# Eleven small rows packed into one array: one transfer in place of eleven

## The reference

```python
m = jax.nn.silu(c) @ w_mod[l] + b_mod[l]
sh1, sc1, g1, sh2, sc2, g2 = jnp.split(m[:, None, :], N_MOD, axis=-1)
mc = jax.nn.silu(c_ctx) @ w_mod[l] + b_mod[l]
...
hx = modulate(x, norm_attn_pre[l], sh1, sc1)      # rms_norm(x, g) * (1 + scale) + shift
hc = modulate(ctx, norm_attn_pre[l], csh1, csc1)
px = hx @ w_in[l]
pc = hc @ w_in[l]
...
x = x + g1 * rms_norm(mix_x, norm_attn_post[l])
hx2 = modulate(x, norm_ffn_pre[l], sh2, sc2)
yx = moe(...)
x = x + g2 * rms_norm(yx, norm_ffn_post[l])
```

## Time and profile before

| what | value |
|---|---|
| median of 3 runs | 1950.54 us |
| lowest and highest | 1948.37, 1951.08 us |
| the profiled execution's time | 1948.93 us |
| its span, first to last instruction | 1947.0 us |
| TensorE busy | 1855.7 us (95%) |
| VectorE, ScalarE busy | 392.5 us (20%), 343.6 us (18%) |
| moved by the DMA engines | 558.16 MB, mean 287 GB/s |

### The profile page before, as it was taken

The page is one execution under the profiler, slowest core; times in us unless marked ns, Lnnn a source line. Parts: engine busy times, 40 slices in busy tenths (PEclk is TensorE's granted clock), DMA queues, the critical chain, the costliest instruction groups (busy, mean ns, idle before and its releaser), DMA issues. The chain is left out here.

```text
span 1947.0 us, 21918 instructions
## 1 busy us (share of the span) xinstructions
PE 1855.7 (95%) x8913; PEld 1054.1 (54%) x8914; DVE 392.5 (20%) x818; ACT 343.6 (18%) x675; POOL 5.3 (0%) x10
## 2 busy tenths in 40 slices
PE   6999799999999999999999997999999999999998
PEld 4757333333333333333333335768888886786664
DVE  1754411011101111111110114542000033110001
ACT  2222311111111111111111113332000032120001
POOL 0000000000000000000000000000000000000000
PEclk9999799999999999999999999999999999999999
DMA  9984399999999999979999999434244413314331
GB/s 393 310 208 156 150 422 428 429 427 430 427 430 428 429 429 427 429 307 429 428 429 427 430 425 312 164 129 172 102 173 172 167 49 130 130 44 173 124 135 65
DMA packets 100582, 558.16 MB, mean 287 GB/s; under 512 B 16600, under 2 KB 33469, under 8 KB 73789
## 3 DMA queue, kind: packets, MB, share of 16 engines
q1 hardware_dynamic: 98084, 553.09, 70.0%
q10 hardware_dynamic: 2458, 4.50, 1.8%
HBM read 552.34 MB, written 5.23 MB: 286 GB/s over the span
## 5 line engine op out<-in xcount | busy, mean ns | idle before, releaser
L1285 PE MATMUL ps<-ring,xs 128*64 128x512 f32 x2112 | 472.4, 594 | 28.4 <-DMA ring<-in_w_up 17.4
L1285 PEld LDWEIGHTS ps<-ring,xs 128*64 128x64 f32 x2112 | 148.5, 137 | 340.6 <-issue 269.2
L1337 PE MATMUL ps<-ring,actT 128*64 128x512 f32 x1056 | 233.9, 595 | 0.0
L1993 PE MATMUL ps<-hT,ring 128*128 128x256 f32 x1024 | 223.9, 379 | 0.2 <-ACT hT L1522 0.2
L1993 PEld LDWEIGHTS ps<-hT,ring 128*128 128x128 f32 x1024 | 194.5, 190 | 29.5 <-issue 2.9
L1337 PEld LDWEIGHTS ps<-ring,actT 128*64 128x64 f32 x1056 | 72.9, 137 | 158.7 <-issue 131.9
L1788 PE MATMUL ps<-hT,ring 128*128 128x256 f32 x512 | 120.2, 391 | 5.8 <-ACT hT L1522 4.7
L1397 DVE TENSOR_SCALAR g<-ps 128x512 f32<-128x512 f32 x33 | 22.8, 691 | 457.5 <-PE ps L1285 457.5
L2003 PE MATMUL ps<-wide,ring 128*128 128x256 f32 x512 | 111.7, 379 | 0.0
L2016 PE MATMUL ps<-ring,wide 128*128 128x512 f32 x256 | 111.0, 592 | 0.0
L1788 PEld LDWEIGHTS ps<-hT,ring 128*128 128x128 f32 x512 | 97.7, 195 | 23.6 <-issue 9.1
(11 more groups left out here) (416 smaller groups left out, 1490.8 us busy)
## 6 DMA issues: line engine op xcount, KB each, us to landing
ring<-in_w_up SPq DMA_DIRECT2D x64, 2048.0 KB, 25.1
ring<-in_w_down SPq DMA_DIRECT2D x64, 2048.0 KB, 22.1
ring<-in_w_gate SPq DMA_DIRECT2D x64, 2048.0 KB, 24.1
ring<-in_mlp_w SPq DMA_DIRECT2D x32, 2048.0 KB, 8.7
ring<-in_w_mod SPq DMA_DIRECT2D x8, 2048.0 KB, 16.3
ring<-in_odd_w_in SPq DMA_DIRECT2D x6, 2048.0 KB, 9.1
ring<-in_w_mod SPq DMA_DIRECT2D x8, 1024.0 KB, 14.5
ring<-in_even_w_in SPq DMA_DIRECT2D x4, 2048.0 KB, 16.7
```

What stands on the lines that cost most here:

```text
L1285: mm = pe.matmul(ps[SLOTS * half:SLOTS * (half + 1), bank, :], xs[:, c % 4, c // 4 * SLOTS:(c // 4 + 1) * SLOTS], m.ring[:, 8 * part + c, ...
L1337: mm = pe.matmul(ps[SLOTS * half:SLOTS * (half + 1), Y, :], actT[:, f % 4, f // 4 * SLOTS:(f // 4 + 1) * SLOTS], m.ring[:, 16 + f, half * ...
L1993: mm = pe.matmul(ps[:, UP[layer][b] + f // 2, (f % 2) * SEQ:(f % 2 + 1) * SEQ], mlp_w1[b][:, c, f * P:(f + 1) * P], hT[:, c, :], start=(c ...
```

## The change

The host packs the eleven arrays into one of 101 x 128 in the order of `ROWS`, and ScalarE loads it with one transfer in place of eleven. TensorE's wait for the rows counts 16 (one transfer) where it counted 16 for each of eleven. All else, the constants' transfer ahead of it, the tile `rows` and what is computed from it, stays.

```diff
+ROW_SOURCE = {"c": "c", "cctx": "c_ctx", "bmod": "b_mod", "pre": "norm_attn_pre", "mix": "mix_norm_2", "mlp": "mlp_norm_2",
+              "qlat": "norm_q_lat", "kvlat": "norm_kv_lat", "post": "norm_attn_post", "ffn": "norm_ffn_pre", "fpost": "norm_ffn_post"}
+
+def packed_rows(arrays):
+    out = np.zeros((NROWS, P), np.float32)
+    for name, (at, n) in ROWS.items():
+        out[at:at + n] = arrays["in_" + ROW_SOURCE[name]].reshape(-1, P)[:n]
+    return out
...
-            pe.wait_ge(rows_in, 16 * len(ROWS))
+            pe.wait_ge(rows_in, 16)
...
-            for name, src in (("c", t["c"]), ("cctx", t["c_ctx"]), ("bmod", t["b_mod"]), ("pre", t["norm_attn_pre"]),
-                              ("mix", t["mix_norm_2"]), ("mlp", t["mlp_norm_2"]), ("qlat", t["norm_q_lat"]),
-                              ("kvlat", t["norm_kv_lat"]), ("post", t["norm_attn_post"]), ("ffn", t["norm_ffn_pre"]),
-                              ("fpost", t["norm_ffn_post"])):
-                at, n = ROWS[name]
-                act.dma_start(rows[at:at + n, :], bass.AP(src.tensor, 0, [[P, n], [1, P]])).then_inc(rows_in, 16)
+            act.dma_start(rows[0:NROWS, :], t["rows"]).then_inc(rows_in, 16)
...
+    arrays["in_rows"] = packed_rows(arrays)
+    t["rows"] = nc.dram_tensor("in_rows", (NROWS, P), F32, kind="ExternalInput").ap()
```

## The result

The changed kernel takes 1968.11 us (median of 4 runs, 1967.72 to 1970.37) beside 1950.38 us before (median of 4, 1948.37 to 1951.08): a ratio of 1.0095, interval [1.0077, 1.0112], or 15 to 22 us more. Forecast were 1967 us and slower. The profiled execution took 1970.37 us with a span of 1968.5 us, 21.5 us over the span of the profiled execution before; the medians are 17.7 us apart.

The account below looks back on a forecast made before the run. SyncE's load queue was taken to bound the start, TensorE the rest. 20.0 - 1.0 - 1.9 - 0.4 = +16.7 us gave 1967 us against the median; range 1962 to 1972.

Parts of the forecast that it names:

- step 1: ScalarE at the start: ten issues go, 4.1 us of issue time, Square at 6.3 us instead of 7.22; worth nothing.
- step 2: The rows' transfer: 101 is prime, so all 101 rows go to one DMA engine.
- step 3: The rows' landing: 102 turns on one engine from 4.8 us, landed at 32.1 us instead of 12.1, 20 us later.
- step 4: The rows' engine: about 2.3 us more work, w_mod's last piece at 28.5 us, w_in's first about 34; hidden.
- step 5: TensorE behind the rows' wait: 20 us less 1.0 in L410 and 1.9 at L422, 17.1; clock 0.4 off; transposes unchanged.
- the bound of 3 us: In the forecast's bounds: up to 3 us if the long rest or ScalarE's issue of 101 rows costs something new.
- step 6: Loads behind moda_ps: b_mod in at about 64.5 us instead of 55.2; no new wait, up to 0.2 us gained.
- rows spread over many engines: Rival on the rows' transfer: rows land near 7.5 us, 1950.2 us, no change; chance 0.07.
- many rows to a turn: Rival: one engine takes many rows a turn, rows at 7.5 to 9.5 us; +2.3 us, 1952.8; chance 0.07.
- the early start: Rival: rows at 7 us and the start moves up with them; 1946 us or less; chance 0.01.
- the delay would be hidden: Rival: TensorE room behind 50 us swallows part of the 17 us; no separate chance given.

Follow-up runs that it names:

- E1: Changed kernel with the packed array padded to 112 rows (16 x 7), still one transfer; 1949.26 us, ratio 0.9997 to the kernel before.
- six counts: Runs with the rows' transfer at 112, 100 and 1 (two transfers), 116, 111, 106 and 101 rows; ratios to the kernel before 0.9997, 0.9996, 1.0006, 1.0014, 1.0041, 1.0095.
- E5: Changed kernel, but SyncE issues w_mod only when the 101 rows have landed; 1955.38 us, ratio 1.0024 to the kernel before.
- E6: Changed kernel with each w_mod block in two transfers of 128 x 4 KB instead of one of 8 KB; 1958.22 us, ratio 1.0040 to the kernel before.
- E4: Changed kernel with the packed array padded to 106 rows (2 x 53), one transfer; ratio 1.0041 to the kernel before, +8.0 us.
- E10: Changed kernel with the packed array padded to 111 rows (3 x 37), one transfer; ratio 1.0014 to the kernel before, +2.7 us.
- E9: Changed kernel with the packed array padded to 116 rows (4 x 29), one transfer; ratio 1.0006 to the kernel before, +1.2 us.
- E7: Changed kernel with the 101 rows' transfer issued by SyncE ahead of x, on w_mod's queue; 1952.37 us, ratio 1.0010 to the kernel before.
- E8: Changed kernel with 60 unused products on TensorE ahead of the wait for the rows; 1963.37 us, ratio 1.0063 to the kernel before.

## Why the prediction was right

The direction, the mechanism and the size came as forecast. In the trace the terms that were off did not cancel: the shift is 19.1 to 19.4 us where the sum had 16.7. That the median came out only 1.1 us above 1967 is in part luck, since the medians are 17.7 us apart and the profiled executions 21.5.

- *ScalarE's issues (step 1)*: worth nothing, shown. Square at 6.35 us (6.3 forecast); E1, with early rows too, ends where the kernel before does.
- *One engine (step 2)*: shown by 102 packets, one of them a completion, and by the six counts.
- *The time to land (step 3)*: 33.0 us against 32.1 forecast. That a turn costs the packet which passes is shown by E5 and E6 and by the steps of the packets. The turns themselves were sized right, 27.0 us measured and 26.9 worked out. What was short is the start, 5.36 us instead of 4.8, and the landing behind the last packet, 0.66 us instead of 0.4. The row's own 0.02 us did not follow from the rows as I read them: by the packet records the 22 turns before ran from 4.79 to 11.52 us, 0.306 us each, which is no more than an 8 KB packet's 0.309. E5 shows it, with 0.024 us from row to row. Of the padded ones E4 landed at 21.6 us (22 forecast), E10 at 17.3 (16.6), E9 at 15.2 (13.7).
- *Load on that engine (step 4)*: hidden here, about 2 us where uncovered (E7).
- *TensorE behind the wait (step 5)*: rows 20.9 us later; plus 1.7 us, as the second transposes took 3.65 us instead of 1.94; less 1.2 us in L410 (1.0 forecast), less 1.75 us of w_in's wait (1.9 forecast): 19.6 us at the first product with w_in, where I had 17.1. **This is the term that was mis-sized:** I credited the clock with 0.4 us and called the transposes unchanged. The credit was 0, the stretch at half clock came again, and the clock, which rose only at 41.83 us, cost 1.7 us that I had only inside the bound of 3 us. Each of these is read from one profiled execution. E8 has both: without the rest 3.4 us less in the transposes and 1.7 us less in L434.
- *Nothing else late (step 6)*: b_mod released VectorE at 67.76 us (64.5 forecast); 2.3 us of the difference are that `moda_ps` came later than worked out. VectorE then had its eight additions done at 77.5 us, TensorE began the transposes of the context at 77.58, and VectorE's part of the context waited 2.00 us for these:

```profile
79.53 1.90 DVE L941 TENSOR_SCALAR zone<-ps,gain,modv 128x256 f32<-128x256 f32 x4 [2.00 <-PE ps L405]
```

  No new wait on TensorE, by a margin of 2 us where I had 2.6. The gain of up to 0.2 us that I named is there: the products behind it take 7.17 us instead of 7.45, which brings the 19.6 us down to 19.4.
- *The end*: the medians are 17.7 us apart, and the ratio's interval is 15.0 to 21.8 us; 16.7 was the sum, and 19.1 is what the trace carries to the experts. The times can't tell these apart.

Of the rivals, rows spread over many engines is excluded by the 102 packets, many rows to a turn by the 27.0 us and by E6, and the early start is E1: it is there and pays nothing. That the delay would be hidden is excluded by the shift of 19.4 us at 98 us and 19.1 at 256 us. The Trainium skill's other statement (same page, "Queues, rings and completion order": some 9 to 17 descriptors before a switch) does not hold for these two queues: the rows' steps in the changed kernel and in E6 fit one packet a turn.

## What to carry to other kernels

Before small transfers are merged, look at the number of rows (partitions) of the result: in the six counts here it decided how many DMA engines work, and the prime 101 left one. Eleven more rows of zeros made the merged transfer land 25 us earlier. A small transfer on few engines that shares them with a stream of large packets waited one large packet for each of its own, so its time to land can be estimated as its rows on one engine times the *other* queue's packet. And a merged transfer saves time only where the end really waits for it.

## What the runs showed that I had not expected

When TensorE's clock rises does not follow from the place in the work. The first group of transposes took 3.16 to 3.68 us in every kernel but E8. The second took 1.94 us before, in E1 to E6, in E8 and in E9, but 3.65 us in the changed kernel, in E7 and in E10. The trace's list of the granted clock agrees each time:

| kernel | first instruction of TensorE, us | first rise to full clock, us | second group of transposes from, us | it took, us |
|---|---|---|---|---|
| before | 12.13 | 15.95 | 17.41 | 1.94 |
| E9 | 15.18 | 19.73 | 20.46 | 1.94 |
| E4 | 21.61 | 24.55 | 26.54 | 1.94 |
| E6 | 22.61 | 27.07 | 27.89 | 1.94 |
| E7 | 6.30 | 20.73 | 15.60 | 3.65 |
| E10 | 17.27 | 26.58 | 22.56 | 3.65 |
| changed | 33.02 | 41.83 | 38.31 | 3.65 |

It is not the length of the rest alone: rows at 17.27 us (E10) had the slow second group, rows at 21.61 (E4) and 22.61 us (E6) did not. Likewise the products with w_in ran 26.10 us in E4 and E10 but 24.41 in E6, behind the same 1.33 us of wait: E6 has no fall of the clock there, E4 has one at 38.21 us. The two together are 3.4 us of the start, and I have no run that says what sets them. With one profiled execution of each kernel it is not even shown that they belong to the kernel and not to the execution: the one of E6 was the fastest of its five, 1953.41 us with a median of 1958.22.
